# FFN gate and up products: both halves' 512-column products first, then both halves' 256-column products

## What is computed

```python
def swiglu(h, w_in, w_out):
    a, b = jnp.split(h @ w_in, 2, axis=-1)
    return (jax.nn.silu(a) * b) @ w_out

for i in range(DEPTH):
    ...
    x = x + MACARON_W * gate[:, 0, None] * swiglu(h, ffn_w_in[i, 0], ffn_w_out[i, 0])
    ...
    x = x + MACARON_W * gate[:, 2, None] * swiglu(h, ffn_w_in[i, 1], ffn_w_out[i, 1])
```

## Time and profile before

| | us |
|---|---|
| median of 3 runs | 3143.48 |
| lowest, highest of the 3 | 3143.33, 3153.83 |
| span of the profiled execution | 3143.0 |
| PE busy in it | 3035.9 (97%) |
| DVE busy | 2373.7 (76%) |
| ACT busy | 1399.3 (45%) |

### The profile page before, as it was taken

The page is one execution under the profiler, slowest core; times in us unless marked ns, Lnnn a source line. Parts: engine busy times, 40 slices in busy tenths (PEclk is TensorE's granted clock), DMA queues, the critical chain, the costliest instruction groups (busy, mean ns, idle before and its releaser), DMA issues.

```text
span 3143.0 us, 49807 instructions
## 1 busy us (share of the span) xinstructions
PE 3035.9 (97%) x19866; PEld 2672.7 (85%) x19866; DVE 2373.7 (76%) x3501; ACT 1399.3 (45%) x2222; POOL 97.0 (3%) x187
## 2 busy tenths in 40 slices
PE   7998999999999999999999999999999999999998
PEld 6886789888888888888896888887788888989887
DVE  6978865988877867879867887877854866765685
ACT  4534122544535753545444554544122544465453
POOL 0000000000000000000000000000000000000000
PEclk9999999999999999999999999999999999999899
DMA  8774433676676335675664666672301553443453
GB/s 348 255 292 151 154 112 124 235 266 250 244 267 230 114 120 231 240 282 212 259 238 150 248 245 251 236 262 81 134 1 62 201 184 135 165 161 141 161 184 131
DMA packets 69670, 609.47 MB, mean 194 GB/s; under 512 B 7728, under 2 KB 7888, under 8 KB 31824
## 3 DMA queue, kind: packets, MB, share of 16 engines
q1 hardware_dynamic: 42768, 459.41, 39.2%
q0 software_dynamic: 26352, 144.88, 12.3%
q10 hardware_dynamic: 336, 2.13, 0.2%
HBM read 604.30 MB, written 2.10 MB: 193 GB/s over the span
## 4 chain that ended last, share of the span: by engine, by line
PE 86%; DVE 9%; ACT 2%; DMA 1%; issue 1%; SPq 0%; DVEq 0%; POOLq 0%; ACTq 0%
PE psum L323 27%; PE psum L926 23%; PE psum L930 12%; PE psum L947 10%; PE psum L954 6%; PE psum L321 4%; PE psum L951 2%; PE psum L1698 1%; DMA weights<-in_weights 1%; DVE arena L812 1%; DVE ada_sum L505 1%; DVE arena L2315 1%; DVE wkv_base L2076 1%; DVE small L2075 1%; PE psum L1631 0%
## 5 line engine op out<-in xcount | busy, mean ns | idle before, releaser
L877 ACT ACTIVATE unit_high<-weights 128x1024 fp32r<-128x1024 f32 x594 | 628.7, 1060 | 709.0 <-PE psum L930 390.4
L883 DVE TENSOR_TENSOR unit_low<-weights,unit_high 128x1024 fp32r<-128x1024 f32 x594 | 725.4, 1223 | 199.9 <-ACT unit_high L877 199.3
L926 PE MATMUL psum<-h_part,unit_high 128*128 128x512 f32 x3168 | 821.5, 396 | 22.3 <-DVE h_part L799 14.7
L926 PEld LDWEIGHTS psum<-h_part,unit_high 128*128 128x128 f32 x3168 | 576.7, 191 | 131.0 <-issue 17.1
L930 PEld LDWEIGHTS psum<-h_part,unit_low 128*128 128x128 f32 x3168 | 445.6, 192 | 29.5
L930 PE MATMUL psum<-h_part,unit_low 128*128 128x256 f32 x3168 | 467.0, 284 | 0.0
L323 PEld LDWEIGHTS psum<-in_part,w_part 128*128 128x128 f32 x2784 | 348.1, 196 | 22.3 <-ACT arena L1205 11.3
L323 PE MATMUL psum<-in_part,w_part 128*128 128x256 f32 x2784 | 361.0, 290 | 6.3 <-issue 3.0
L947 PE MATMUL psum<-hidden,unit_high 128*128 128x512 f32 x1386 | 353.8, 396 | 0.0
L1053 DVE TENSOR_REDUCE arena<-psum 128x256 f32<-128x512 f32 x396 | 272.6, 688 | 60.0 <-PE psum L930 48.5
L505 DVE SCALAR_TENSOR_TENSOR ada_sum<-ada_in,c_act,ada_sum 128x1536 f32<-128x1536 f32 x154 | 278.6, 1812 | 22.9 <-DMA ada_in<-in_ada_w 22.8
(11 more groups left out here) (314 smaller groups left out, 2795.8 us busy)
## 6 DMA issues: line engine op xcount, KB each, us to landing
weights<-in_weights SPq DMA_DIRECT2D x290, 1536.0 KB, 6.5
ada_in<-in_ada_w POOLq DMA_DIRECT2D x182, 768.0 KB, 5.9
consts<-in_consts POOLq DMA_DIRECT2D x1, 1700.0 KB, 16.9
x<-in_x SPq DMA_DIRECT2D x1, 1024.0 KB, 8.7
v_first<-arena ACTq DMA_DIRECT2D x1, 1024.0 KB, 5.7
arena<-v_first ACTq DMA_DIRECT2D x1, 1024.0 KB, 4.8
weights<-in_weights SPq DMA_DIRECT2D x1, 512.0 KB, 5.5
out<-x SPq DMA_DIRECT2D x1, 512.0 KB, 2.6
```

The source lines that it names most:

```text
L877: k.nc.scalar.activation(k.unit_part[0][:, n % UNIT_RING], w, ACT.Copy).then_inc(k.sem["unit_high"], 1)
L883: k.nc.vector.tensor_tensor(k.unit_part[1][:, n % UNIT_RING], w, k.unit_part[0][:, n % UNIT_RING].bitcast(FP32), ALU.subtract).then_inc(k. ...
L926: mm(k.psum[:, 2 * (j % 2) + half, :].rearrange("p (i t) -> p i t", i=2), lhsT=part(2 * j + half, 0, t), rhs=k.h_parts[:, :, t], start=t = ...
```

## The change

```diff
@@ -978,6 +978,7 @@
                 pe.wait_ge(sem["gate_up_read"], 2 * (FT * i + j - 2) + half + 1)
             for t in range(KT):
                 up_high(j, half, t)
+        for half in range(2):
             for t in range(KT):
                 up_low(j, half, t)
     for v in range(FT):
```

## The result

| | median us | runs | lowest to highest |
|---|---|---|---|
| before | 3146.63 | 22 | 3143.09 to 3153.83 |
| after | 3152.37 | 22 | 3145.37 to 3160.58 |

The ratio is 1.0020, 95% interval 1.0013 to 1.0026: the change makes the kernel slower by 6 us, where the prediction said 0.2 us. The time itself lies at the upper end of the range given, but 3.2 us of it are the base: with 22 runs the median of before is that much above the one of three runs on which the prediction stood. The profiled execution after has a span of 3153.4 us and a time of 3155.14 us, 1.7 us more than its span. The change adds a line to the program, so what stands behind it has a line number one higher in the kernel after: L1054 is L1053 of before, L1009 (ACT's square of a tile of x) is L1008, and L1068 and L1069 (DVE's update of x) are L1067 and L1068.

The account below looks back on a forecast made before the run. PE was taken to bound the kernel. Profiled span 3143.0 - 3.2 (switches) + 1.6 + 1.8 (waits) = 3143.2, plus 0.5 from span to median: 3143.7 us, range 3139.0 to 3152.5, 80%.

Parts of the forecast that it names:

- What bounds the kernel; the tile's price: Up stages: PE alone bounds, busy 97% of the span; a half takes 2.79 us, a tile 5.58 us.
- The term of the switches: 189 tiles: one start of a 512-column run less per tile, 0.017 us each, 3.2 us off; range -4.7 to +1.5 us.
- rivals 3 and 4: All tiles: long runs of 512-column products slow, 3165 us, 4%; or long runs shed the excess, 3064 us, 2%.
- The two waits: PE waits for DVE at FFN 0's gate products, 1.6 us, and FFN 1's modulation rows before tile 13, 1.8 us.
- rival 1: FFN 0 and FFN 1: DVE has unseen slack, no new waits, only the switches tell; 3140.3 us, 8%.
- Units never late: Running stages: tightest unit, unit 7 of FFN 1, keeps 0.3 us of 3.06 us cover; costed at nothing.
- The sign for DVE: In the profile after, DVE starts the sum of half 1 without a wait in every tile.
- The last hidden tile: End of FFN 1's up stage: cover before v = 2 shrinks from 2.67 to 0.7 us; costed at nothing.
- Rival 2: Last hidden tile late in each of 8 FFNs, DVE one chunk (1.8 us) later than worked out: +8.8, 3152.5 us, 6%.
- The clock: After the two new PE gaps: low clock counted zero, with up to 1.7 us for each in the range.
- The base: Whole kernel before: profiled span 3143.0 us, median 0.5 us above the span.

Follow-up runs that it names:

- the spread chunks: New order in FFN 1 alone, three of the twelve chunk sums of its down stage one v later, against the kernel before: ratio 1.0004.

## Why the prediction was wrong, point by point

- **What bounds the kernel; the tile's price.** Right. The term of the switches, 0.017 us a tile, was 0.02 (123.53 against 123.95 us for 21 tiles, sixteen products in 3.65 and 1.91), and rivals 3 and 4, other paces of a long run, are both refuted by it.
- **The two waits.** Right in place and size: 1.57 us (1.6 said) and 1.72 us (1.8 said). This refutes rival 1.
- **Units never late.** Right: no wait of PE for L883 in any FFN's running stage. The sign for DVE came true as well: it starts the sum of half 1 without a wait in all 198 tiles, where before it waited in 84.
- **The last hidden tile.** The sentence held and the step failed. v = 2 waits for nobody, since the hidden tile is ready at 689.81, 1.0 us ahead of it, as the timeline of the kernel after shows:

```profile
689.39 0.42 DVE L1094 TENSOR_TENSOR hidden<-arena,hidden 128x256 fp32r<-128x256 f32 x1
...
690.82 0.40 PE L947 MATMUL psum<-hidden,unit_high 128*128 128x512 f32 x1
```

But I asked of DVE's lateness only whether the one thing next due would be late, and the rest was "Costed at nothing". The 1.7 us went on into the down stage, where DVE's first business is chunk sums whose end lets the next transfers start. **This is the step that failed**, with its neighbour: of the DMAs I costed only the weight stream (slots freed later, 11.2 us of cover) and not the chunk stream, whose requests move with each chunk sum, in a stage where the DMA engines were 99% busy and one chunk landed 0.02 us ahead of its use. That price is 5.8 us in down and norm of FFN 1: 2.7 us of wait, 2.5 of the sixteen products at the lower clock, and the rest the sums of squares ahead of them. The ratio falls from 1.0026 to 1.0005 where the entry is on time. Late entry without the wait at tile 13 measured less, 1.0006 to 1.0014.
- **Rival 2** was the nearest, one chunk of lateness in a down stage. It looked in the wrong place (v = 2, in eight FFNs) and so was given the wrong price. That its 3152.5 us is nearly the measured 3152.37 is luck: there is no wait at v = 2 in any FFN, the loss is in one stage of one FFN, and 3.2 us of the time are the base.
- **The clock.** I counted zero for the two waits with up to 1.7 us each. At tile 13 no low clock follows in any profile; at FFN 0 a longer stretch is seen, but kernels without the wait show the like. The third wait, which I did not see, brings one in each of the four profiles that have it at 2.3 us or more, and at 1.83 us in one profile and not in another at 1.85. "The clock falls where it did not before" was one of my own signs of being wrong, and it came.
- **The base.** The median of before is 3146.63 us with 22 runs, not 3143.48. The half microsecond that I put between span and time is 1.7 to 1.8 in every execution whose span and time are both known. Neither changes the ratio.

## What to carry to other kernels

When a change makes an engine late that is off the critical path, follow its lateness until it is gone, not only to the next thing that waits for it; what it releases (a buffer, and with it a transfer) counts as waiting too, and the worst place is where the DMA engines are full. A stage whose transfers are just in time has a price for lateness that no row of waits shows beforehand: look for landings close to their use. And an engine's wait costs by what is queued behind it: moving three chunk sums one unit later brought the ratio from 1.0026 to 1.0004 though DVE's waits grew longer.

## What the runs showed of the hardware

- The extra time at the start of a run of 512-column products doesn't grow with the run of 256-column products ahead of it: 3.65 us for sixteen against 1.84 for eight, 1.91 against 0.95.
- With two streams on full DMA engines (386 to 391 GB/s in FFN 1's down stage) a transfer of 768 KB, of which the shortest in this stage take 4.4 us, took up to 9.8 us there in the kernel after and 11.2 us with the spread chunks; with the new order in FFN 1 alone the last of sixteen pieces landed 5.25 us after the eighth; in before, the same chunk's last piece came 2.0 us after its fifteenth.
- A wait of PE of 2.7 us amid dense work was followed by 0.50 of clock for some us (eight products in 3.62 us instead of 1.84), one of 1.72 us was not, and of two of 1.83 and 1.85 us in the same place one was and one wasn't.
